# First expert's gate product: for all tokens during the routing, or on gathered rows after it

## The reference

```python
def moe_swiglu(h, w_router, w1, w3, w2):
    logits = jnp.einsum('bsd,de->bse', h, w_router)
    top_val, top_idx = lax.top_k(logits, TOP_K)          # 2 of 8 experts
    top_gate = jax.nn.softmax(top_val, axis=-1)
    gates = jnp.sum(jax.nn.one_hot(top_idx, N_EXPERTS) * top_gate[..., None], axis=-2)
    for e in range(N_EXPERTS):                           # width 3584 each
        y = y + gates[..., e:e + 1] * swiglu(h, w1[e], w3[e], w2[e])
# swiglu(h, w1, w3, w2) = (silu(h @ w1) * (h @ w3)) @ w2
```

## Time and profile before

| | |
|---|---|
| median of 3 runs | 1494.01 us (1493.68 to 1502.43) |
| the profiled execution | 1492.68 us |
| its span, first to last instruction | 1490.9 us |
| mean granted clock of TensorE | 0.995 |
| busy: PE, DVE, ACT | 98%, 77%, 64% |
| moved by DMA | 438.96 MB, 294 GB/s over the span |

### The profile page before, as it was taken

How to read it: one execution, slowest core, us unless ns; L and a number is a source line. 1 busy time by engine, 2 the same in 40 slices (tenths; PEclk the granted TensorE clock), 3 DMA queues, 4 the chain that set the end, 5 groups by cost and what they waited for, 6 DMA issues and landing times.

```text
span 1490.9 us, 19196 instructions
## 1 busy us (share of the span) xinstructions
PE 1456.6 (98%) x7278; PEld 1223.4 (82%) x7278; DVE 1146.7 (77%) x973; ACT 957.9 (64%) x857; POOL 33.6 (2%) x21
## 2 busy tenths in 40 slices
PE   6999999999998999999999999999999999999997
PEld 6999788888887788888888888888888888888885
DVE  5886645554386498988889888888888998888894
ACT  6645444433386466776777777777676777777773
POOL 0000000000000000000000001000000000000000
PEclk9999999999999999999999999999999999999999
DMA  9610636545352469999999999999999999999992
GB/s 334 213 71 1 248 119 235 209 175 194 115 174 72 167 245 382 393 365 387 382 384 381 387 368 380 392 362 375 386 374 355 392 393 366 396 387 368 373 383 90
DMA packets 185277, 438.96 MB, mean 294 GB/s; under 512 B 5904, under 2 KB 7312, under 8 KB 185232
## 3 DMA queue, kind: packets, MB, share of 16 engines
q1 hardware_dynamic: 180496, 426.11, 77.3%
q0 software_dynamic: 2704, 9.96, 2.4%
q10 hardware_dynamic: 2032, 2.28, 0.5%
HBM read 432.04 MB, written 6.29 MB: 294 GB/s over the span
## 4 chain that ended last, share of the span: by engine, by line
PE 85%; issue 7%; DVE 3%; DMA 3%; ACT 1%; POOL 0%; ACTq 0%; DVEq 0%; SPq 0%; POOLq 0%
PE ps L261 26%; PE ps L263 26%; PE ps L262 26%; DVE wlo L250 2%; DMA raw<-in_od_moe_w 2%; PE ps L446 1%; PE ps L915 1%; DMA out<-arena,slot_tok 1%; PE ps L924 1%; DMA gains<-in_gains 1%; PE ps L1521 1%; PE ps L1460 0%; PE ps L1962 0%; PE ps L1129 0%; ACT whi L244 0%
## 5 line engine op out<-in xcount | busy, mean ns | idle before, releaser
L250 DVE TENSOR_TENSOR wlo<-raw,whi 128x2048 fp32r<-128x2048 f32 (+1 forms) x408 | 910.5, 2273 | 159.5 <-ACT whi L244 157.2
L244 ACT CAST whi<-raw 128x2048 fp32r<-128x2048 f32 (+1 forms) x407 | 752.5, 1899 | 181.9 <-DMA raw<-in_od_moe_w 108.4
L261 PE MATMUL ps<-whi,hThi 128*128 128x512 f32 (+1 forms) x1240 | 489.3, 395 | 1.3 <-DVE hTlo L305 1.3
L263 PE MATMUL ps<-whi,hTlo 128*128 128x512 f32 (+1 forms) x1240 | 481.8, 389 | 0.0
L262 PE MATMUL ps<-wlo,hThi 128*128 128x512 f32 (+1 forms) x1240 | 481.0, 388 | 0.0
L263 PEld LDWEIGHTS ps<-whi,hTlo 128*128 128x128 f32 x1240 | 232.8, 188 | 49.2
L261 PEld LDWEIGHTS ps<-whi,hThi 128*128 128x128 f32 x1240 | 233.0, 188 | 48.0 <-issue 2.2
L262 PEld LDWEIGHTS ps<-wlo,hThi 128*128 128x128 f32 x1240 | 233.2, 188 | 46.0 <-issue 0.5
L261 PE MATMUL ps<-whi,aThi 128*128 128x512 f32 x560 | 219.3, 392 | 1.4 <-DVE aTlo L438 1.4
L263 PE MATMUL ps<-whi,aTlo 128*128 128x512 f32 x560 | 218.4, 390 | 0.0
L262 PE MATMUL ps<-wlo,aThi 128*128 128x512 f32 x560 | 217.9, 389 | 0.0
(11 more groups left out here) (289 smaller groups left out, 812.0 us busy)
## 6 DMA issues: line engine op xcount, KB each, us to landing
raw<-in_od_moe_w SPq DMA_DIRECT2D x168, 2048.0 KB, 9.2
raw<-in_ev_ffn_w SPq DMA_DIRECT2D x21, 2048.0 KB, 7.9
raw<-in_ev_w_in SPq DMA_DIRECT2D x6, 2048.0 KB, 10.3
raw<-in_ev_w_out SPq DMA_DIRECT2D x2, 2048.0 KB, 8.3
raw<-in_od_w_in SPq DMA_DIRECT2D x2, 2048.0 KB, 7.7
raw<-in_od_w_out SPq DMA_DIRECT2D x2, 2048.0 KB, 8.1
raw<-in_ev_w_in SPq DMA_DIRECT2D x2, 1024.0 KB, 8.8
xres<-in_x SPq DMA_DIRECT2D x2, 512.0 KB, 4.3
```

Of the source, the lines that this page charges most:

```text
L244: act.copy(whi[s][:, part], raw[s][:, part]).then_inc(hi_ready, 1)
L250: dve.tensor_tensor(wlo[s][:, part], raw[s][:, part], whi[s][:, part].bitcast(F32), ALU.subtract).then_inc(lo_ready, 1)
L261: pe.matmul(to, lhi, rhi, start=first, stop=False)
L263: return pe.matmul(to, llo, rhi, start=False, stop=last)
```

## The change

`dense` and its four portions leave PE's program, and with them `gather_silu` on PE, the two activations, the copy and the split order around them on ACT, and the special multiplication on DVE. Expert 0's first block takes the same path as every other one: both products on gathered rows, `act_silu`, `dve_gate`. On ACT the cast of `U_MOE + 3`, whose first half stood ahead of the split of the gathered rows, now comes whole after the activation. DVE's order is the same: the gate, then the split of `U_MOE + 3`.

```diff
             def moe(q):                                  # ACT
                 if q == 0:
-                    act.wait_ge(unit_used, U_MOE + 1)
-                    for t in range(TT):
-                        act.activation(sil[:, t, :], H1[t][:, :], ACT.Silu, scale=rs[:, t:t + 1]).then_inc(first_sil, 1)
-                    split_hi(act, U_MOE + NS, 0, uses(0, 0) + 1, halves=(0,))
                     gathered(0, FIRST)
-                    act.wait_ge(sil_ps, 1)
-                    act.copy(sil_slots, H3[1][:, :]).then_inc(sil_ready, 1)
-                    split_hi(act, U_MOE + NS, 0, uses(0, 0) + 1, halves=(1,))
+                    act_silu(act, 1, U_MOE, gates(0, 0, 0))
+                    split_hi(act, U_MOE + NS, 0, uses(0, 0) + 1)
...
-                    dve.wait_ge(unit_used, U_MOE + 2)
-                    dve.wait_ge(sil_ready, tiles(0, 0, 0))
-                    dve.tensor_tensor(actf[:, 0, :], sil_slots, H3[0][:, :], ALU.mult).then_inc(a_ready, 1)
+                    dve_gate(dve, 1, U_MOE + 1, gates(0, 0, 0))
                     split_lo(dve, U_MOE + NS, 0)
...
-            def dense(t, ks):
-
-                wh, wl = band(whi[0], KD, GW), band(wlo[0], KD, GW)
-                tok = slice(t * P, t * P + P)
-                for k in ks:
-                    if t == 0 and k % 4 == 0:
-                        pe.wait_ge(lo_ready, 2 * U_MOE + k // 4 + 1)
-                    ins = product(pe, H1[t][:, :], hThi[:, k, tok], hTlo[:, k, tok], wh[:, k], wl[:, k],
-                                  k == 0, k == KD - 1)
-                return ins
...
-                if b < 3:
-                    dense(0, (2 * b, 2 * b + 1))
             ins.then_inc(unit_used, 1)
-            dense(0, (6, 7))
             pe.wait_ge(rt_rows, 1)
             for t in range(TT):
                 ins = pe.transpose(ps[5][:, t * NE:t * NE + NE], by_expert[:, t * P:t * P + P], ident[0:NE, 0:NE])
             ins.then_inc(rt_ps, 1)
-            dense(1, early)
...
             ins.then_inc(rank_ps, 1)
-            dense(1, late).then_inc(unit_used, 1)
...
                     gather_first()
                     index(0, 0)
-                    gather_silu()
                     pe.wait_ge(xglo_ready, 2)
+                    pe_up(pe, u, 0, H1[0])
                     pe_up(pe, u + 1, 1, H3[0])
```

More of the change, by code:

```diff
@@ L1577, in build_program @@
         by_expert = Psel[0:NE].rearrange("p t i -> p (t i)")
-        rt_rows, rt_ps, first_sil, sil_ps = sem("rt_rows rt_ps first_sil sil_ps")
-        sil_slots = actf[:, 1, :]
+        rt_rows, rt_ps = sem("rt_rows rt_ps")
         def slots_of(t):
@@ L1905, in experts_tensor @@
             pe_turn_x(pe, 3, 1)
-            def dense(t, ks):
-                wh, wl = band(whi[0], KD, GW), band(wlo[0], KD, GW)
-                tok = slice(t * P, t * P + P)
-                for k in ks:
-                    if t == 0 and k % 4 == 0:
-                        pe.wait_ge(lo_ready, 2 * U_MOE + k // 4 + 1)
-                    ins = product(pe, H1[t][:, :], hThi[:, k, tok], hTlo[:, k, tok], wh[:, k], wl[:, k],
-                                  k == 0, k == KD - 1)
-                return ins
-            early, late = range(KD // 2), range(KD // 2, KD)
             s = U_ROUTER % NS
@@ L1973, in gather_first @@
                 ins.then_inc(xg_ps, 1)
[L1975 to L1980, removed]
             def down_product(g, u, s, first, last):
```

## The result

The changed kernel takes 1503.85 us in the median of 15 runs (1497.35 to 1514.38), the kernel before 1496.99 in its 15 (1492.43 to 1506.97). The ratio is 1.0050 with a 95% interval of 1.0030 to 1.0071: slower by 7.5 us (4.5 to 10.6). The profiled execution took 1502.38 us with a span of 1500.5, 9.6 more than the span before. The forecast of +5.3 us lies inside that interval, but the forecast of "same" with a chance of 0.94 does not fit it: the change is a slowdown clear of noise.

What follows compares the result with a forecast made beforehand. PE is 98% busy, but around the routing its small products wait for DVE's chain. Product +5.44, routing -1.3, dense product ahead of gather -0.9, slow clock +2.1 give +5.3 us: 1499.3, range 1495.5 to 1504.

Steps and rivals of the forecast that it cites:

- "same": Whole kernel: measured time not told apart from the kernel before; chance 0.94, against 0.01 faster and 0.05 slower.
- the step from the sum to the class: Whole kernel: a measurement can tell about 1%, 15 us, from no change, so only larger slowdowns count as slower.
- The removed products lay beside the chain: Around the routing: the removed 1.8 us activation gather and other 9 us of products save no time.
- rival C: Routing: PE's own work sets the time, so the change saves 7.3 us, giving 1486.7; chance 0.04.
- The routing: Router to slot selection: selection 1.3 us earlier, ACT's exponential ending DVE's wait; gather also spared 0.9 us behind a dense product.
- The gather at half clock: Gather's 32 passes after the routing: TensorE partly at half clock, ending 2.1 us later than at full pace.
- First product: Behind the gather: first product on gathered rows starts at 533.1 us, against 533.26 before.
- The first product's own 5.44 us: Behind the gather: the added 24 matmuls run at full pace and add 5.44 us.
- rival B: Behind the gather: 2.0 us idle keep the clock low into the first product; +8.8 us, 1502.8; chance 0.22.
- All later links shift together: From first product to end: each link as before but about 5.3 us later, the 0.52 us stall at 590.41 unchanged.
- rival E: Weight transfers: a 6 us queue gap is missed later, the stall at 590.41 growing up to 5.3 us; 1504.6; chance 0.05.
- both its early places: Before 15.07 and at 80.30 us in the old trace: granted clock 0.50, full again 3.0 and 5.1 us later.

Runs made afterwards that it cites:

- The second execution: The changed kernel profiled once more, unaltered, against its own first execution: 1500.93 us, router to gate 32.81 us, 2.06 less than in the first.

## Why the prediction was right or wrong

It had the mechanism and the direction of the time (+5.3 us forecast, +7.5 measured, 4.5 to 10.6). Two of its steps failed.

The first is the step from the sum to the class: "A measurement of this kernel can tell about 1% from no change, 15 us", and from it 0.94 on "same". No working is given for that figure. The measured interval is 0.2% to either side, so its own +5.3 us would have been a slowdown by 0.35%, outside such an interval, and the measured 0.50% (0.30 to 0.71) is a clear slowdown, to which it gave 0.05.

The second is a term of the sum: the product added behind the gather was put at 5.44 us, full pace, with nothing for the clock after the idle time ahead of it. It took 7.17 us in the profiled execution, and 5.6 in the second. The median of before had moved too: 1494.01 in 3 runs, 1496.99 in 15.

- **The removed products lay beside the chain**: right. Of 12.7 us taken from PE nothing but 2.1 us of routing came free (gather begun at 14.00 instead of 16.13), and rival C (faster, 1486.7) was far off: the first product would have had to start before 16.4 and starts at 21.6 to 22.1.
- **The routing**: right to 0.1 us at most steps. Copy at 5.27 (5.3 forecast), L1765 at 6.15 (6.3), the exponential the last of DVE's waits, selection done at 13.9 (13.9), gather begun at 14.0 (14.0).
- **The gather at half clock**: right. Forecast 5.7 us (from 3.0 to 5.1 us of half clock), measured 5.9 and 5.4, with 4.7 and 3.7 us of half clock; 5.0 with 2.8 us in the kernel with the product twice. The price of a slow pass, 0.214 us, came from L357 between 7.3 and 10.5 us. The clock is on record only from 11.3 us on in that trace, so that row showed a pace and not its cause; the gather of the changed kernel has the same 0.214 at a granted clock of 0.50.
- **First product**: 22.06 and 21.60 against 21.7.
- **The first product's own 5.44 us**: here the sum was short. It took 7.17 in the profiled execution, since the clock fell a second time. That was rival B, to which I gave 0.22 of a chance and no part of the sum. B had it nearly right in kind (the wait behind the gather) and too dear: +8.8, where the gather was to run all slow as well; the stretch shows +7.2. The second execution shows +5.16, near the forecast, because the second fall did not come in it; that was chance. A better sum would have added half of the 1.7 us, since the fall came in one of two executions of this kernel, and in one of two other kernels with that wait and a first product behind it.
- **All later links shift together**: right in three profiles, 951.8, 952.1 and 952.2 us from gate to end with 0, 1 and 2 added products. Against rival E speaks the doubled product. The other six profiles took 953.5 to 956.6; one of them, 953.6, has the path of the kernel before, so at least 1.8 us of that comes without the change.

The Trainium skill's page TensorE: Matmul & The Clock Gate (section Why this matters for your kernels) warns of idle gaps between bursts. The long waits here bear it out: in all three executions that had the waits of about 2.8 and 3.4 us unfilled the clock fell, at 518.6, 518.9 and 520.0 us. The prediction called both its early places cases of the rule; only the one before 15.07 is an idle stretch, at 80.30 PE was issuing one-column matmuls. The wait of 1.66 us behind the gather is shorter than the gaps that the rule names, and in the four executions that had it unfilled the clock fell in two and stayed in two, so here the measurement decides. That this wait makes the clock fall is likely and not proved: in the three executions that had it filled no fall came there, which two falls in four alone could also give.

What stays open: gate to end took 951.8 to 956.6 us over nine profiles, 4.8 us between the kernel with filled waits and the kernel before. All do the same work there. Their traces show 0 to 2.4 us of waits of PE, at other places in each (one wait of 1.4 us near the end, which all share, is left out). The transfers go with it. The median load landed 9.2 us after its issue in the first two profiles and 9.6 to 9.9 in the seven later ones. ACT waited for weight units, from 560 us to 1480, for 106 and 108 us in the first two and 142 to 187 in the others. The unaltered changed kernel stands on both sides, with 952.06 and 954.9 us from gate to end. So the pace of the transfers differs between executions whatever the kernel, and 2.8 of the 4.8 us come without any edit; that the slower transfers are their cause is likely, but no run varied them. Whether a lead of PE over the transfers adds waits, so that a part of what filled waits gain is given back, nine executions do not show.

## What to carry to other kernels

Work on the busiest engine that lay beside a chain of waits was free here, and a product moved from there to behind the chain cost its full price: find the chain's length without the cover before counting what is removed. In this kernel matmuls that fill waits also held TensorE's clock; if they must go, look for the next burst after each wait and price it at half speed. Where an effect is a few microseconds, compare marks inside the profiles on both sides of the change, take the same kernel's profile twice, and work out what the timed runs can tell apart from their own spread.

## What the hardware showed that I had not expected

The clock explains much of when the router starts, though the work ahead of it is the same in all nine. In the four executions whose clock stayed full from 92 us to the router it started at 511.24 to 511.97; in the five whose clock fell at least once on the way, at 513.42 to 517.31.

In the changed kernel's first execution TensorE ran at half clock from 184.1 to 187.5, a place between two stages at which the profile of the kernel before has the full clock. In the kernel with the filled wait behind the gather it was at half clock from 464.6 to 468.0 and from 481.6 to 491.8, and its router started at 517.31, 5.9 us later than in the kernel before. Ahead of 464.6 stands a wait of PE of 1.76 us; all nine executions have it, and in four of them the clock fell within 3 us of its end. So short waits are followed by half clock in some executions of the same work and not in others, here too. The clock does not explain all: of 15 executions of the changed kernel five have a mean granted clock of 0.990, with spans from 1498.1 to 1507.8 us.

Useless matmuls made the stretch shorter: 36 of them, 8.2 us of TensorE's time, took 1.7 to 3.8 us off it. And in the kernel with the old products unused a wait of 1.66 us behind a gather at full clock (3.6 us), itself preceded by full work, was followed by half clock from 536.1: the following product's matmuls from 536.23 on start 0.427 us apart instead of 0.227.
